# A flow-matching trunk layer on one core: 64 instead of 32 latent tokens served from gathered expert rows, with the low parts, gate chunks and one number row rearranged

## The chip, the cores and the metric

The kernel is written for Trainium2 and runs on one core. The metric is the device time of one execution in microseconds, median of several. The profile is one further execution, with one row for each instruction of each engine: PE (TensorE matmuls), PEld (its weight loads), DVE (VectorE), ACT (ScalarE), POOL (GpSimd) and SP (SyncE, which only issues DMAs).

## What is computed

One trunk layer over 128 context tokens and 512 latent tokens of width 1024, then a final norm: a recurrent and a pooling branch, merged and projected, then a "PEER" channel mixer that picks, for each token, 128 of 16,384 experts (8 heads, 16 each). The mixer is what the change touches:

```
e = (take_along_axis(i1, ci // 16) * 128 + take_along_axis(i2, ci % 16))     # 8 heads x 16 experts a token
g = softmax(sc)
ub = take(u_tab, eb)                       # (token, 128, 1024)
act = gelu(einsum('cd,ced->ce', xb, ub))
vb = take(v_tab, eb)
out = einsum('ce,ced->cd', gbk * act, vb)
```

## The kernel before, in words

All activations lie feature by feature, tokens along the free axis. After the mixer the program goes through these stages:

**Queries and scores** (to about 697 us): 16 blocks of `wq`, scores against the keys, and on VectorE a top-16 `search` for each pair of head (8) and tile of 128 tokens (5), with a `select` that turns indices into expert numbers.

The experts are then served in two ways. *Gathered*: for the 128 context tokens and the first `KS` = 32 latent tokens the rows of the chosen experts are fetched by indirect DMA. A gather fetches one row of 4 KB for each of 128 partitions (512 KB). A context token takes one partition and 128 gathers; the 32 latent tokens are laid four slots to a gather, and take 32 more. So `NG` = 160 gathers of `u_tab` rows, each followed on VectorE by a dot product with the token (`dots`, `early_dots`), and later 160 gathers of `v_tab` rows, each added with its weight to a sum (`weigh`). *Dense*: for the other `TD` = 480 latent tokens all 16,384 experts are computed, 128 at a time, and what was not chosen gets a gate of zero.

**U stage.** For each of 128 blocks of experts (`expert_scores`) PE runs 24 matmuls: 8 slices of the contraction times three products (high x high, low x high, high x low: numbers are split in a high and a low part). ACT rounds the raw weights to the high part (`w_hi`), and POOL or DVE makes the low part `wLo` (`low`). ACT puts a GELU on the result and writes it to a scratch tensor in HBM (`gelu_out`: `gel_d`, two buffers of `gel`, each refilled only when its previous write has landed). A block n's `w_hi` is made as block n-2 ends.

- The first `U1` = 68 blocks run while DVE still searches. POOL makes their low parts, and between them issues the first `D1` = 80 gathers, in program order: 4 gathers to 3 blocks. A gather waits until the row buffer (one of `UR` = 8) has been dotted. DVE puts dots between the pieces of the search.
- Then ACT does the softmax's exponential, DVE the rest of it, PE transposes the expert numbers. 
- In the last `U2` = 60 blocks PE also builds the dense gates: `gates_of` multiplies for each token two one-hot matrices (`ohA`, `ohB`, from `one_hots` on DVE), 8 tokens to a block. ACT copies the result to `stage`, and after 8 blocks (a chunk of 64 tokens) writes 4 MB to HBM (`gate_scratch`), on the same queue as its GELU writes. Six chunks go to HBM; the last 12 blocks' gates (96 tokens) stay in `stage`. DVE here makes the low parts too, and dots 4 rows for 3 blocks, while POOL only issues gathers, up to 8 rows ahead.

**V stage.** For each of 128 blocks DVE multiplies GELUs (`gsr`) and gates (`gates4`, and `stage` for what was kept), ACT and DVE split the product into high and low, and PE again runs 24 matmuls of 480 columns (`values`) that add up in PSUM. DVE also adds 5 gathered rows to 4 blocks.

**The end:** sums, residual, final norm.

Queues: SP loads raw weights (512 KB a block, four buffers), and in the V stage GELUs and gates. ACT's queue writes GELUs and gate chunks. POOL's queue gathers.

Of the kernel before, what the change touches and what calls it, by code (L numbers as in the profile page):

```python
# [152 lines left out]
def build(nc, xT, posT, cT, vecs_d, iota_d, invc_d, gw_d, pw_d, keys_d, wblk, ublk, u_tab, v_tab, ident_d, iota128_d, gel_d, gate_d, yT, st_out):  # L153
# [25 lines left out]
    gates4 = [sb("gates4a", [128, 6, 4, 64])]  # L179
# [21 lines left out]
    same = sb("same", [128, KS])  # L201
# [5 lines left out]
    gates4.append(sb("gates4b", [128, 6, 4, 64]))  # L207
# [86 lines left out]
    iotaP, i1P = P[3][:, 1, 0:16], P[3][:, 1, 16:16 + SLOTS].rearrange("p (a c) -> p a c", a=2)  # L294

# [69 lines left out]
    def _(sp_):  # L365
# [45 lines left out]
        def gate_rows(i, half, n):  # L411

            sp_.dma_start(gates4[half][:, :, :, :].rearrange("p c n t -> p c (n t)"),
                          gate_out[0:6, :, ds(i * 8 + n, 4), :].rearrange("c p n t -> p c (n t)")).then_inc(gt_ld[half], 16)
# [3 lines left out]
        for h in range(2):  # L418
            sp_.wait_ge(gate_st[h], 16 * 3)
            sp_.wait_ge(gel_st[h], 16 * 2)  # L420
# [38 lines left out]
    def _(pool):  # L459
# [45 lines left out]
        with pool.Fori(0, D1 // 16) as i:  # L505
            for b in range(12):
                low(i, 12, 8 + b)
                for g in range(b * 4 // 3, (b + 1) * 4 // 3):
                    if g % 8 == 0:
                        indices(i, 2, i * 16 + g, g // 8, 0, 8, g // 8 + 1)  # L510
                    gather(i, 16, g + 1, g % UR, g // 8, g % 8, u_tab)
        with pool.Fori(0, (SLOTS - D1) // 16) as i:
            for g in range(16):
                if g % 8 == 0:
                    indices(i, 2, i * 16 + (D1 + g), g // 8, 0, 8, (D1 + g) // 8 + 1)
                gather(i, 16, D1 + g + 1, g % UR, g // 8, g % 8, u_tab)
        pool.wait_ge(s["e_ready"], 2)
        for seq in range(SLOTS, NG):
            if seq % 8 == 0:
                indices(0, 0, seq, seq // 8 % 2, 0, 8, seq // 8 + 1)  # L520
            if seq < NG - 16:
                gather(0, 0, seq + 1, seq % UR, seq // 8 % 2, seq % 8, u_tab)
            else:
                gather(0, 0, seq + UR - VR + 1, seq % VR, seq // 8 % 2, seq % 8, u_tab)
        with pool.Fori(0, NE // 16) as i:
            for half in range(2):
                indices(i, 4, i * 16 + half * 8, half, 0, 8, 0, last=False)
                indices(i, 4, i * 4 + (SLOTS + half * 2), half, 8, 2, NG // 8 + half * 2 + 2)
                for g in range(8):
                    v = half * 10 + g + g // 4  # L530
# [1306 lines left out]
```

## Time and profile before

| | |
|---|---|
| time, median of 3 runs | 2189.85 us (2189.37 to 2190.43) |
| the profiled execution: time, and span from first to last instruction | 2194.28 us, 2192.5 us |
| mean granted TensorE clock | 0.979 of full speed |
| busy: PE, PEld, DVE, ACT, POOL | 96%, 86%, 74%, 36%, 33% |
| chain that ended last, by engine | PE 78%, DVE 13%, DMA 3%, issue 3%, ACT 2% |

The chain follows the work back from the last instruction to what released it each time, so its shares say where time was decided, while the busy shares are averages over stages that have different limits. Matmul records overlap one another, so the time from one matmul to the next is read from counts in a stretch or from the chain, not from a row's mean.

### The profile page before, as it was taken

The page shows a single profiled execution, that of the slowest core. Times are in us where ns is not written, and L with a number is a line of the kernel's source. Part 1 is how long each engine was busy: PE and PEld are TensorE (multiplying, and loading weights), DVE is VectorE, ACT ScalarE, POOL GpSimd, SP SyncE. Part 2 cuts the span into 40 slices and gives each one's busy share as a digit, 9 for nine tenths or more (in the row PEclk, how much of TensorE's full clock was granted, in tenths as well). Part 3 has the DMA queues.
Part 4 walks back from the last instruction along what each step waited for, and adds up shares of the span by engine and source line. Part 5 has one row for each costly group of instructions (what it writes and reads, how often), then busy time and mean ns, then how long its engine had stood idle before and what let it go on. Part 6 is the DMA issues. An engine that isn't in the chain of part 4 may idle for free.

```text
span 2192.5 us, 34766 instructions
## 1 busy us (share of the span) xinstructions
PE 2111.8 (96%) x11708; PEld 1879.1 (86%) x11708; DVE 1630.6 (74%) x3336; ACT 799.9 (36%) x1046; POOL 725.6 (33%) x524
## 2 busy tenths in 40 slices
PE   6889998999999999999999999999999999999998
PEld 2889998998899888778888889888888888888887
DVE  4539998242589599993788888887777777777787
ACT  2435555222423322222454445553232323232322
POOL 1223232323133666667422122121222322332331
PEclk8899999999899999999999999999999999999998
DMA  9211222434412688878877677677989989889893
GB/s 368 96 54 58 68 63 68 183 126 169 168 59 78 216 283 279 260 243 284 289 285 285 248 272 292 227 279 245 320 302 313 312 309 367 307 310 317 305 339 115
DMA packets 167482, 502.10 MB, mean 229 GB/s; under 512 B 16608, under 2 KB 74336, under 8 KB 165600
## 3 DMA queue, kind: packets, MB, share of 16 engines
q1 hardware_dynamic: 101872, 273.96, 36.5%
q0 software_dynamic: 46080, 167.79, 22.2%
q10 hardware_dynamic: 19440, 59.25, 6.8%
q8 instruction: 43, 0.70, 0.1%
q14 instruction: 47, 0.39, 0.1%
HBM read 436.45 MB, written 64.50 MB: 228 GB/s over the span
## 4 chain that ended last, share of the span: by engine, by line
PE 78%; DVE 13%; DMA 3%; issue 3%; ACT 2%; SPq 1%; POOL 0%; ACTq 0%; DVEq 0%; POOLq 0%
PE P L840 30%; PE P L557 22%; PE P L751 17%; PE P L775 4%; DMA gel_scratch<-gel 2%; PE P L654 1%; DVE rows L1524 1%; DVE rowsX L1524 1%; PE P L580 1%; DVE oh L1555 1%; DVE oh L1562 1%; DVE keysel L1566 1%; PE P L716 1%; PE P L612 1%; DMA modraw<-in_wblk 1%
## 5 line engine op out<-in xcount | busy, mean ns | idle before, releaser
L864 ACT ACTIVATE wHi<-raw 128x1024 fp32r<-128x1024 f32 x330 | 346.3, 1049 | 1219.9 <-PE P L840 459.4
L751 PE MATMUL P<-hHi,wHi 128*128 128x480 f32 x1024 | 396.1, 387 | 10.8 <-POOL wLo L479 8.1
L751 PE MATMUL P<-hLo,wHi 128*128 128x480 f32 x1024 | 389.3, 380 | 0.0
L751 PE MATMUL P<-hHi,wLo 128*128 128x480 f32 x1024 | 389.1, 380 | 0.0
L1631 DVE TENSOR_TENSOR wLo<-raw,wHi 128x1024 fp32r<-128x1024 f32 x188 | 230.2, 1225 | 167.0 <-ACT wHi L864 162.6
L473 POOL TENSOR_TENSOR wLo<-raw,wHi 128x1024 fp32r<-128x1024 f32 (+1 forms) x76 | 185.2, 2437 | 453.9 <-ACT wHi L864 446.6
L496 POOL DMA_INDIRECT rows<-in_v_tab,Eg x160 | 175.2, 1095 | 468.6 <-DVE accB L1679 225.4
L557 PE MATMUL P<-hHi,wHi 128*128 128x320 f32 x960 | 229.1, 320 | 18.9 <-DVE hLo L1216 14.0
L751 PEld LDWEIGHTS P<-hHi,wHi 128*128 128x128 f32 x1024 | 193.5, 189 | 43.8 <-issue 15.8
L557 PE MATMUL P<-hLo,wHi 128*128 128x320 f32 x960 | 221.1, 311 | 0.0
L557 PE MATMUL P<-hHi,wLo 128*128 128x320 f32 x960 | 220.8, 311 | 0.0
L751 PEld LDWEIGHTS P<-hHi,wLo 128*128 128x128 f32 x1024 | 193.0, 189 | 30.2
L751 PEld LDWEIGHTS P<-hLo,wHi 128*128 128x128 f32 x1024 | 193.5, 189 | 28.2
L840 PE MATMUL P<-wfHib,wLo 128*128 128x480 f32 x512 | 195.0, 381 | 0.0
L840 PE MATMUL P<-wfLob,wHi 128*128 128x480 f32 x512 | 194.9, 381 | 0.0
L840 PE MATMUL P<-wfHia,wHi 128*128 128x480 f32 x512 | 194.2, 379 | 0.0
L840 PE MATMUL P<-wfHib,wHi 128*128 128x480 f32 x512 | 194.1, 379 | 0.0
L840 PE MATMUL P<-wfHia,wLo 128*128 128x480 f32 x512 | 193.5, 378 | 0.0
L840 PE MATMUL P<-wfLoa,wHi 128*128 128x480 f32 x512 | 192.3, 376 | 0.0
L479 POOL TENSOR_TENSOR wLo<-raw,wHi 128x1024 fp32r<-128x1024 f32 x68 | 163.5, 2404 | 79.7 <-ACT wHi L864 79.3
L557 PEld LDWEIGHTS P<-hHi,wHi 128*128 128x128 f32 x960 | 162.9, 191 | 25.4 <-issue 16.5
L496 POOL DMA_INDIRECT rows<-in_u_tab,Eg x88 | 94.8, 1077 | 235.8 <-DVE rows L1524 169.9
(250 smaller groups left out, 3761.2 us busy)
## 6 DMA issues: line engine op xcount, KB each, us to landing
raw<-in_ublk SPq DMA_DIRECT2D x128, 512.0 KB
raw<-in_v_tab SPq DMA_DIRECT2D x128, 512.0 KB
raw<-in_wblk SPq DMA_DIRECT2D x104, 512.0 KB
gel_scratch<-gel ACTq DMA_DIRECT2D x128, 240.0 KB
gsr<-gel_scratch SPq DMA_DIRECT2D x128, 240.0 KB
gate_scratch<-stage ACTq DMA_DIRECT2D x6, 4096.0 KB
gates4a<-gate_scratch SPq DMA_DIRECT2D x16, 768.0 KB
gates4b<-gate_scratch SPq DMA_DIRECT2D x16, 768.0 KB
```

The lines of the kernel that those rows point to most:

```text
L473: pool.tensor_tensor(wLo[:, g % 2, 0:kk], raw[:, r, 0:kk], wHi[:, g % 2, 0:kk].bitcast(f32), ALU.subtract).then_inc(raw_used[r], 1)
L479: pool.tensor_tensor(wLo[:, n % 2, :], raw[:, n % 4, :], wHi[:, n % 2, :].bitcast(f32), ALU.subtract).then_inc(raw_used[n % 4], 1)
L496: pool.indirect_dma_start(out=row(n), out_offset=None, in_=tab, in_offset=bass.IndirectOffsetOnAxis(ap=Eg[:, buf, at:at + 1], axis=0)).the ...
L557: last = nc.tensor.matmul(P[g % 2][:, h, 0:HALF], w_[:, g % 2, k * 128:(k + 1) * 128], cols(x_, k, h), start=(st and a == 0 and b == 0), s ...
L580: last = nc.tensor.matmul(parts_of(m)[32 * j:32 * j + 32, :], c32[:, k, :], raw[:, n % RAW, k * 128:(k + 1) * 128], start=(a == 0), stop=( ...
L612: last = nc.tensor.matmul(P[r // 4][0:2, r // 2 % 2, r % 2 * 256:r % 2 * 256 + 256] .rearrange("p (a n) -> p a n", a=2), cvec[:, 2 * k:2 * ...
L751: last = nc.tensor.matmul(P[0][:, j % 2, 0:TD], w_[:, j % 2, k * 128:(k + 1) * 128], x_[:, k, C0:T], start=(k == 0 and a == 0 and b == 0), ...
L775: last = nc.tensor.matmul(P[1][:, q, n * 128:(n + 1) * 128], ohB[:, q, n, :], ohA[:, q, n, :], start=True, stop=True)
L840: last = nc.tensor.matmul(P[k // 2][:, k % 2, 0:TD], w_[:, j % 2, k * 128:(k + 1) * 128], x_[j % 2][:, :], start=(first and a == 0 and b = ...
L864: return nc.scalar.activation(out, in_, f, **kw)
L1524: V.scalar_tensor_tensor(out=row(b), in0=row(b), scalar=1.0, in1=vec, op0=ALU.mult, op1=ALU.mult, accum_out=actv[:, ds(i * per + n, 1)]).t ...
L1631: V.tensor_tensor(wLo[:, n % 2, :], raw[:, n % 4, :], wHi[:, n % 2, :].bitcast(f32), ALU.subtract).then_inc(raw_used[n % 4], 1)
```

## The change

- `KS` goes from 32 to 64, so 448 latent tokens stay dense instead of 480. The 64 are laid two slots to a gather: 64 gathers instead of 32 for each table, `NG` = 192.
- `U1`/`U2` go from 68/60 to 72/56, `D1` from 80 to 96. POOL issues 3 gathers to 2 blocks in the first part.
- In the second part the low parts move from DVE to POOL, which alternates them with the gathers; the loops are written out. DVE there builds one-hots and dots only (96 dots in 56 blocks).
- The row of numbers 0 to 127 that `ohB` compares with is read from PSUM (`iota128P`, in bank P3); the token vectors are read from PSUM (`htokP`, P2) to the last dot, so the first matmul of the V stage that writes P2 waits for `act_ready`, which DVE gives after the last dot.
- Seven chunks of gates; five go to HBM, the last two (chunks 5 and 6, 128 tokens) stay whole in `stage`.
- In the search, dots start after the second tile's row numbers and not after the first's; then 2 follow each unit (before 1 and 2 in turn), and 5 lie in each `select` (before 3).

```diff
-KS = 32
+KS = 64
-U1, U2 = 68, 60
+U1, U2 = 72, 56
-D1 = 80
-KEPT = 48
+D1 = 96
+CH, CK = 7, 5
...
-        with pool.Fori(0, D1 // 16) as i:
-            for b in range(12):
-                low(i, 12, 8 + b)
-                for g in range(b * 4 // 3, (b + 1) * 4 // 3):
+        with pool.Fori(0, D1 // 48) as i:
+            for b in range(32):
+                low(i, 32, 8 + b)
+                for g in range(b * 3 // 2, (b + 1) * 3 // 2):
...
+        for b in range(U2):
+            low(0, 0, U1 + b)
+            for seq in range(D1 + b * (NG - D1) // U2, D1 + (b + 1) * (NG - D1) // U2):
+                if seq == SLOTS:
+                    pool.wait_ge(s["e_ready"], 2)
...
             for k in ((4, 5, 6, 7, 2, 3, 0, 1) if first else range(KC)):
+                if first and k == 4:
+                    pe.wait_ge(s["act_ready"], 1)
...
+        def gates_of_chunk(c):
+
+            half = (c + 1) % 2
+            if c >= 2:
+                act.wait_ge(gate_st[half], c // 2 * 16)
+            if c < CK:
+                with act.Fori(0, 2) as i:
+                    for j in range(4):
+                        gate_block(i + c * 2, j, half, i * 32 + j * 8)
+                act.wait_ge(s["bank_free"], c * 16 + 18)
+                act.dma_start(gate_in[c, :, :], stage[:, half, :, :].rearrange("p n t -> p (n t)")
+                              ).then_inc(gate_st[half], 16)
+            else:
+                for b in range(8):
+                    gate_block(c * 2 + b // 4, b % 4, half, b * 8)
...
             search(n, unit, before)
-            early_dots(1 + n % 2)
+            early_dots(2)
...
         dotted[1] = D1
-        early_dots(4)
-        low(0, 0, P_U + U1, 0)
-        early_dots(2)
-        low(0, 0, P_U + U1, 1)
-        with dve.Fori(0, (SLOTS - D1) // 16) as i:
-            one_hots(i, htokP)
-        one_hots(3, htok2[:, :])
-        one_hots(4, htok2[:, :], final=True)
+        early_dots(6)
+        for b in range(U2):
+            one_hots(b)
+            for n in range(D1 + b * (NG - D1) // U2, D1 + (b + 1) * (NG - D1) // U2):
+                late_dot(n)
...
         def weighs(i, c):
 
-            weigh(i, c + c // 4, acc if c % 2 == 0 else accB, wgt[:, ds(i * 16 + c, 1)])
-            if c % 4 == 3:
-                weigh(i, c + c // 4 + 1, acc2, wgt[:, ds(i * 4 + (SLOTS + c // 4), 1)])
+            weigh(i, c + c // 2, acc if c % 2 == 0 else accB, wgt[:, ds(i * 16 + c, 1)])
+            if c % 2 == 1:
+                weigh(i, c + c // 2 + 1, acc2, wgt[:, ds(i * 8 + (SLOTS + c // 2), 1)])
```

What the code above makes of the engines' order is seen at two places. On POOL, at the end of the first part of the U stage, the program before leaves the low parts (`wLo`) and goes on with gathers alone (`rows` and `rowsX` are the row buffers, `Eg` the expert numbers of the next eight gathers):

```order
L479 TENSOR_TENSOR wLo<-raw,wHi 128x1024
...
L489 COPY Eg<-E 128x8
L496 DMA rows<-in_u_tab,Eg 128x1024 x4
L496 DMA rowsX<-in_u_tab,Eg 128x1024 x4
L489 COPY Eg<-E 128x8
```

The changed program goes on with a low part for each block, and one or two gathers behind it:

```order
L482 TENSOR_TENSOR wLo<-raw,wHi 128x1024
L492 COPY Eg<-E 128x8
L499 DMA rows<-in_u_tab,Eg 128x1024
L482 TENSOR_TENSOR wLo<-raw,wHi 128x1024
L499 DMA rows<-in_u_tab,Eg 128x1024 x2
L482 TENSOR_TENSOR wLo<-raw,wHi 128x1024
L499 DMA rows<-in_u_tab,Eg 128x1024
L499 DMA rowsX<-in_u_tab,Eg 128x1024
L482 TENSOR_TENSOR wLo<-raw,wHi 128x1024
```

So a gather is now issued behind the low part of its own block, and no longer as soon as a buffer is free. On DVE, at the same place, stood before, between the copies of the transposed numbers and the first one-hot (`P` is PSUM, `actv` the dot's result):

```order
L1625 COPY keysel<-P 128x2x512
L1626 COPY SC<-P 128x512
L1524 SCALAR_TENSOR_TENSOR rows,actv<-rows,P 128x1024 x2
L1524 SCALAR_TENSOR_TENSOR rowsX,actv<-rowsX,P 128x1024 x2
L1631 TENSOR_TENSOR wLo<-raw,wHi 128x1024
L1524 SCALAR_TENSOR_TENSOR rowsX,actv<-rowsX,P 128x1024 x2
L1631 TENSOR_TENSOR wLo<-raw,wHi 128x1024
```

Now there stands:

```order
L1629 COPY keysel<-P 128x2x512
L1630 COPY SC<-P 128x512
L1525 SCALAR_TENSOR_TENSOR rows,actv<-rows,P 128x1024 x2
L1525 SCALAR_TENSOR_TENSOR rowsX,actv<-rowsX,P 128x1024 x4
L1643 TENSOR_TENSOR ohB<-P,keysel 128x512
L1646 TENSOR_SCALAR ohA<-iota,keysel,SC 128x128 x4
L1643 TENSOR_TENSOR ohB<-P,keysel 128x512
L1646 TENSOR_SCALAR ohA<-iota,keysel,SC 128x128 x4
L1525 SCALAR_TENSOR_TENSOR rows,actv<-rows,P 128x1024
```

The low parts are gone from DVE, the six dots are the same, and each block is two groups of one-hots and then its one or two dots.

## Rows read from the trace of the kernel before

**Rows 1.** Windows by stage (U first, U second, V): stretch; busy us (instructions) of PE, PEld, DVE, ACT, POOL; clock; DMA share; GB/s.
```profile
697.00:1074.00 377.00, 366.18 (x1667) 312.69 (x1666) 300.07 (x878) 109.84 (x144) 244.73 (x167) 0.99 0.78 258
1074.00:1502.00 428.00, 419.41 (x2377) 375.82 (x2376) 360.51 (x813) 212.47 (x239) 92.58 (x86) 0.99 0.72 265
1502.00:2168.00 666.00, 666.00 (x3069) 575.84 (x3069) 506.25 (x678) 200.28 (x260) 194.81 (x187) 1.00 0.89 308
```

**Rows 2.** Chain in order of time (start, us, what), U stage.
```profile
1067.43 7.01 PE P L751 x24
...
1225.63 1.78 PE P L775 x16
...
1241.39 5.22 PE P L751 x24
...
1248.32 15.31 DMA gel_scratch<-gel
...
1272.20 5.20 PE P L751 x24
...
1411.93 5.22 PE P L751 x24
...
1441.60 5.20 PE P L751 x24
```

**Rows 3.** Windows of PE for line L557 (320 columns): busy (matmuls), busy (loads).
```profile
200.00:300.00 100.00, 87.65 (x580) 85.41 (x580) 1.00 0.21 67
```

**Rows 4.** Windows of all engines, first part of U.
```profile
720.00:860.00 140.00, 140.00 (x648) 121.16 (x647) 113.08 (x310) 41.01 (x54) 95.77 (x64) 1.00 0.78 262
860.00:1000.00 140.00, 131.86 (x587) 110.21 (x587) 134.03 (x419) 36.44 (x48) 90.43 (x62) 0.99 0.81 259
```

**Rows 5.** POOL's gathers: two of the timeline, and their group in the page.
```profile
738.09 1.12 POOL L496 DMA_INDIRECT rows<-in_u_tab,Eg  x1 [1.14 <-issue]
...
947.02 0.94 POOL L496 DMA_INDIRECT rows<-in_u_tab,Eg  x1 [6.62 <-DVE rows L1524]
...
L496 POOL DMA_INDIRECT rows<-in_u_tab,Eg x88 | 94.8, 1077 | 235.8 <-DVE rows L1524 169.9
```

**Rows 6.** Timeline of ACT, second part of U (L1176 writes a gate chunk).
```profile
1186.55 1.06 ACT L864 ACTIVATE wHi<-raw 128x1024 fp32r<-128x1024 f32 x1 [2.72 <-PE P L751]
...
1244.09 0.34 ACTq L1176 DMA_DIRECT2D gate_scratch<-stage  x1
...
1265.12 0.57 ACT L864 ACTIVATE gel<-P 128x480 f32<-128x480 f32 x1 [3.40 <-issue]
```

**Rows 7.** Windows with the most DMA traffic: second part of U, V.
```profile
1245.00:1260.00 15.00, 15.00 (x86) 13.49 (x85) 12.72 (x32) 7.06 (x8) 2.54 (x2) 1.00 0.99 396
1808.00:1840.00 32.00, 32.00 (x149) 27.68 (x148) 23.70 (x34) 9.32 (x12) 8.88 (x9) 1.00 1.03 402
```

**Rows 8.** Timeline of DVE: its first dot, and a block of the second part.
```profile
743.83 1.22 DVE L1524 SCALAR_TENSOR_TENSOR rows<-rows,P 128x1024 f32<-128x1024 f32 x1 [20.77 <-DMA rows<-in_u_tab,Eg]
...
1190.02 0.69 DVE L1639 TENSOR_TENSOR ohB<-iota,keysel 128x512 f32<-128x512 f32 x1 [1.16 <-ACT stage L864]
1190.63 1.11 DVE L1643 TENSOR_SCALAR ohA<-iota,keysel,SC 128x128 f32<-128x128 f32 x4
...
1193.29 1.21 DVE L1524 SCALAR_TENSOR_TENSOR rowsX<-rowsX,P 128x1024 f32<-128x1024 f32 x1
...
1194.43 1.22 DVE L1524 SCALAR_TENSOR_TENSOR rowsX<-rowsX,P 128x1024 f32<-128x1024 f32 x1
```

**Rows 9.** Timeline: two DVE operations of like size, and a low part on POOL.
```profile
713.62 0.18 DVE L1547 SCALAR_TENSOR_TENSOR abf<-abf 128x16 f32<-128x16 f32 x1
713.83 2.29 DVE L1549 TENSOR_TENSOR ab<-abf 128x16 uint32<-128x16 f32 x1
...
713.68 2.40 POOL L479 TENSOR_TENSOR wLo<-raw,wHi 128x1024 fp32r<-128x1024 f32 x1 [2.79 <-ACT wHi L864]
```

**Rows 10.** Timeline of DVE, V stage.
```profile
1607.96 1.23 DVE L1631 TENSOR_TENSOR wLo<-raw,wHi 128x1024 fp32r<-128x1024 f32 x1 [1.61 <-ACT wHi L864]
```

More of the change, by code:

```diff
@@ L200, in build @@
     stfin = sb("stfin", [128, 2, KC])
-    same = sb("same", [128, KS])
+    same = sb("same", [128, 32])
+    sameK = sb("sameK", [128, KS])
     sp = sb("sp", [128, 16])
@@ L799, in context_sums @@
             for k in range(KC):
-                last = nc.tensor.matmul(P[1][:, 0, k * KS:(k + 1) * KS], acc2[:, k * 128:(k + 1) * 128], same[:, :],
+                last = nc.tensor.matmul(P[1][:, 0, k * KS:(k + 1) * KS], acc2[:, k * 128:(k + 1) * 128], sameK[:, :],
                                         start=True, stop=True)
@@ L1568, in select @@
             ins.then_inc(s["head_done"], 1)
+            early_dots(1)
         def row_numbers(t, selects):
@@ L1603, in _ @@
                         dve.sem_inc(s["row_free"], UR)
-                        dotted[1] = 70
+                    else:
+                        dotted[1] = D1 - 12
             before = unit
@@ L1632, in low @@
                             ).then_inc(raw_used[n % 4], 1)
-        def one_hots(i, vec, final=False):
-            for b in range(12):
-                for q in range(2):
-                    dve.wait_ge(s["bank_free"], i * 24 + (b * 2 + q + 1))
-                    c = i * 96 + (C0 + b * 8 + q * 4)
-                    V.tensor_tensor(ohB[:, q, :, :], iota128[:, :].unsqueeze(1).broadcast_to([128, 4, 128]),
-                                    keysel[:, 1:2, ds(c, 4)].rearrange("p a n -> p (a n)").unsqueeze(2).broadcast_to(
-                                        [128, 4, 128]), ALU.is_equal)
-                    for n in range(4):
-                        last = V.tensor_scalar(ohA[:, q, n, :], iota128[:, :],
-                                               keysel[:, 0:1, ds(c + n, 1)].rearrange("p a n -> p (a n)"),
-                                               SC[:, ds(c + n, 1)], ALU.is_equal, ALU.mult)
-                    last.then_inc(s["oh_ready"], 1)
-                for g in range(b * 4 // 3, (b + 1) * 4 // 3):
-                    dots(i, 16, D1 + g, vec)
-                if not (final and b >= 10):
-                    low(i, 12, P_U + U1, b + 2)
@@ L1652, in _, with one_hots @@
-        dotted[1] = D1
-        early_dots(4)
-        low(0, 0, P_U + U1, 0)
-        early_dots(2)
-        low(0, 0, P_U + U1, 1)
-        with dve.Fori(0, (SLOTS - D1) // 16) as i:
-            one_hots(i, htokP)
-        one_hots(3, htok2[:, :])
-        one_hots(4, htok2[:, :], final=True)
+        def one_hots(b):
+            for q in range(2):
+                dve.wait_ge(s["bank_free"], b * 2 + q + 1)
+                c = C0 + b * 8 + q * 4
+                V.tensor_tensor(ohB[:, q, :, :], iota128P.unsqueeze(1).broadcast_to([128, 4, 128]),
+                                keysel[:, 1, c:c + 4].unsqueeze(2).broadcast_to([128, 4, 128]), ALU.is_equal)
+                for n in range(4):
+                    last = V.tensor_scalar(ohA[:, q, n, :], iota128[:, :], keysel[:, 0, c + n:c + n + 1],
+                                           SC[:, c + n:c + n + 1], ALU.is_equal, ALU.mult)
+                last.then_inc(s["oh_ready"], 1)
```

95 lines of the change are left out of this document (40 added, 55 removed).

## The prediction, made before the change was run

> **What bounds the kernel now.** I read the windows by stage first [rows 1]. PE is busy without a gap in the V stage (666 of 666 us), and in 97 and 98% of the two parts of the U stage. These stages are two thirds of the span, and PE ends them. In their chain there is a steady beat of 24 expert matmuls in 5.20 us, and in the second part of U 16 one-hot matmuls in 1.78 us beside them [rows 2]. So an expert matmul of 480 columns takes 216.7 ns from one to the next.
>
> The gaps come second. From 697 to the first one-hots at 1074.4 (the end of the slow block that starts at 1067.43 [rows 2]) lie 69 blocks, 358.8 us at 5.20; it took 377. Between 860 and 1000 PE did 587 matmuls where 140 us hold 648 [rows 4]: 61 x 0.2167 = 13 us lost. The timeline says how: a gather on POOL waits for a dot on DVE, 6.6 us in the row [rows 5], and the low part behind the gather is late. About 4 of the other 5 us are at the switch to one-hots, where that slow block waited for a low part that DVE owed behind four dots (7.01 us for 24 matmuls). In the second part of U, 60 x 1.78 + 59 x 5.20 = 413.6 us became 428 [rows 1]: 14.4 lost. After a 4 MB gate write ACT's next GELU write lands 15.3 us after its issue [rows 2], and the GELU that needs this buffer waits 3.4 us [rows 6]. Four beats of 6.98 are 27.9 us; around two gate writes they are 30.8 and 29.7 [rows 2].
>
> **The columns.** The change removes 32 of 480 columns from 6,144 matmuls. No row has 448 columns, so I bound the price by 320: 87.65 us for 580 matmuls, 151.1 ns each [rows 3]. The slope is (216.7 - 151.1)/160 = 0.41 ns a column, hence 203.6 ns at 448 (4.89 us a block), and 13.1 ns x 6,144 = **-80.6 us**. The end above is in proportion to the columns: 216.7 x 32/480 = 14.4 ns, -88.8 us. That loads of weights set a floor near 200 ns is excluded, since 320 columns run faster.
>
> **The one-hots.** 56 blocks instead of 60, at 1.78 [rows 2]: **-7.1 us**.
>
> **The first part of U.** POOL must now issue 3 gathers in 2 x 4.89 us instead of 4 in 3 x 5.20: one each 3.26 us, before 3.90. DVE has to dot at that rate, for POOL is at most 8 rows ahead. DVE is full here (134 of 140 us [rows 4]), and by the program it gets 64 dots instead of 54 before the end of the search: 10 x 1.14 us (from one dot to the next [rows 8]) = 11.4 us more. But before, its first dot waited 20.8 us for the first gather [rows 8], since it was asked for too early; now DVE does the second tile first, and that wait is gone. So the search ends some 9 us sooner, while PE is sooner by 50 blocks x 0.31 = 16 us. The balance is about as tight as before: I leave the 13 us where they are (**0**), with -10 to +12 as ends. ACT comes to the exponential when it did (64 x 5.20 = 333 us, 68 x 4.89 = 333 us in). At the switch the low part is POOL's and no dots stand before it; but six dots (6.9 us) and one group of one-hots (1.6) have to fit in two blocks (9.8 us), which leaves 1.3 us for two copies of 1024 and 512 elements, which at the dots' 1.2 ns an element are 1.8. I take 2 us where 4 were: **-2**.
>
> **The second part of U.** DVE sheds a low part (1.2 us a block) and gets 1.71 dots instead of 1.33 (+0.4): 3.27 for its one-hots [rows 8] and 1.71 x 1.14 make 5.2 us of a beat of 6.67, so it isn't the bound; nor is POOL with 2.4 [rows 9] + 1.71 x 1.08 [rows 5] = 4.2 us. What gets worse is the collision with a gate write. A block's traffic without GELUs is 512 KB of weights and 1.71 gathers, 1.42 MB in 6.67 us = 213 GB/s, before 1.22 MB in 6.98 = 175. All queues together moved 396 and 402 GB/s in the fullest windows [rows 7], in the mean 399. The 4.19 MB of a write and the GELU block behind it (0.25, now 0.23 MB) then need 4.44/(0.399 - 0.175) = 19.8 us before, and the trace has 1248.3 + 15.3 - 1244.1 = 19.5 [rows 2, 6]. Now it is 4.42/(0.399 - 0.213) = 23.8 us, if the others keep their pace, while the buffer is wanted 0.6 us sooner. So the wait of 3.4 becomes up to 8 us, and less as a stalled PE asks for less: I take 6. A second wait stands beside it: gathers were issued up to 8 rows (6 blocks) ahead of their dot, and now 8 to 9 us ahead (behind the low part of block n, made as n-2 ends; the dots of n follow one-hots made after n-1 ended). Alone a gather took 743.8 - 738.1 = 5.7 us [rows 5, 8]; behind a gate write it may be as late as a GELU write, 15 us. DVE then stands for some us, at the same time as ACT. I take 6 us for each of 5 writes, 30 us, instead of 9 (of the 14.4; the rest I give to the last gates before V, which keep it): **+21 us**. The ends are +3 (2.4 each, as in the stretches seen) and +40.
>
> **The V stage.** DVE adds 1.5 rows a block instead of 1.25. It waits 1.61 us of a block for ACT's high part when it has one row to add [rows 10]; a second row (1.2 us) comes in each 2nd block and not each 4th, so 0.1 to 0.2 us are left in those when the beat is 4.89, and 1.4 in the others. Two buffers even this out. DMA: 512 + 224 + 160 + 768 KB in 4.89 us are 348 GB/s, before 1584 KB in 5.20 = 312 (308 with the edges [rows 1]). The same stage carried 402 GB/s for 32 us and PE lost nothing (149 matmuls, 215 ns each [rows 7]). So it fits; for bursts I take **+4 us** (0 to +30). The new wait for the last dot at the start of V is covered: after its last gates PE has 4.9 us of one more block, and two dots take 2.3.
>
> The Trainium skill (DMA: Bandwidth & Descriptors, Specifications) puts the limit of one core's HBM traffic at about 358 GB/s; by that rule 348 in V would just fit, and the sum would be the same there, while a gate write would need 4.42/(0.358 - 0.213) = 30 us (an estimate) and each of the 5 waits some 6 us more. The windows at 396 and 402 GB/s disagree with the limit.
>
> **The sum.** -80.6 - 7.1 - 2 + 21 + 4 = **-65 us**. From the profiled execution's 2194.3 this gives 2129; the median is 4.4 lower, so I predict **2125 us**, with 2100 (columns in proportion, small collisions) to 2148 (the worst collisions) for this case alone. Changes under about 0.2% (4 us) can't be told from none.
>
> **The rivals.**
>
> *Waits don't grow* (0.15): collisions stay at 9 us and V at 0. That is -90, 2100. For it: most writes cost little before. Against it: the gathers' shorter lead.
>
> *DMA becomes the bound of V* (0.13). Its share is 0.89 at 308 GB/s [rows 1], in proportion it is full at 346, and 1664 KB (1.70 MB) take 4.93 us a block; with bursts 5.0 to 5.1, +14 to +27 on the sum, 2139 to 2152. Against it: share 1.03 at 402 GB/s [rows 7].
>
> *The gathers' lead is too short in ordinary blocks too* (0.12). Then DVE waits for rows, and PE for `ohA`, in each of 56 blocks; at 0.5 us that is +28, 2153. Against it: 5.7 us of 8.
>
> *Slower: DVE and POOL shut each other out* (0.05). Beside a low part a DVE operation like one of 0.18 us took 2.29, and both ended at 716.1 [rows 9]. Low parts now run beside one-hots in each block. By the rows a low part lies from 1.1 to 3.5 us after a block's end (behind 1.06 of `wHi`), and the first `ohA` starts at 1190.6 - 1186.5 = 4.1 [rows 6, 8]: they miss each other by 0.6 us. If gathers push the low part back, a block pays up to 2.4 us; with 1 us of slack on DVE that is 1.4 x 56 = +78, 2203. It decides from 1.2 us of PE's time a block (65/56).
>
> The Trainium skill (SBUF — State Buffer, the table of ports and its consequences) says that both engines share a pair of ports as an exclusive lock, which VectorE needs for two inputs in SBUF or a double-rate mode; by that rule an `ohA` that comes during a low part waits for its end, as the rows of 716.1 agree, and a dot with its vector in PSUM doesn't.
>
> *The change doesn't do what it says* (0.01): something else holds the beat at 5.2; then -7 - 2 + 21 + 4 are left, 2206.
>
> The forecast has 0.54. The first four cases make 0.94, of which I leave 0.02 to "within 0.2%"; faster 0.92, slower 0.06. The range 2100 to 2153 leaves out the slower cases, half of the first rival and the tails of the second and third, 2 in 10.
>
> **What the new profile would show.** In the chain 24 matmuls in 4.89 us (5.2 would refute the first term) and 16 in 1.78. Some 60 matmuls missing around the search's end, with POOL waiting for dots. After each of five gate writes an ACT wait before a GELU, and a DVE wait for gathered rows; none there, and the collision term is wrong; DVE waits between writes speak for the third rival. In V PE without gaps at a DMA share of 0.95 or more; waits for `wLo` or `wfLo` speak for the second. `ohA` rows of over 1 us each speak for the slower case.

## The result and the profile after

The changed kernel takes 2155.5 us (median of 4 runs, 2153.2 to 2160.1) beside 2189.6 of the kernel before on the same chip: a ratio of 0.985 (0.983 to 0.986), 34 us faster where the prediction had 65. Its profiled execution took 2157.4 us, with a span of 2155.6. In all that follows two executions are left out, one of 7040.9 us of e6_spread_switch and one of 4222.1 us of the kernel before beside it.

Windows of the kernel after, by stage, with the columns of [rows 1]:

```profile
693.00:1076.00 383.00, 365.98 (x1773) 329.16 (x1771) 329.49 (x900) 115.08 (x155) 271.41 (x185) 1.00 0.82 275
1076.00:1495.00 419.00, 385.40 (x2215) 360.18 (x2216) 304.05 (x754) 196.93 (x223) 225.31 (x165) 0.95 0.75 276
1495.00:2134.00 639.00, 634.43 (x3103) 582.57 (x3101) 539.24 (x725) 198.44 (x262) 232.33 (x220) 0.99 0.93 337
```

PE was busy in 98% of the second part of U before and is in 92% now, at a granted clock of 0.95 where it was 0.99. Where it waits, the groups of PE's matmuls say (busy us, mean ns, idle before and what ended it):

```profile
L752 PE MATMUL P<-hHi,wHi 128*128 128x448 f32 x1024 | 383.6, 375 | 16.3 <-POOL wLo L482 13.1 <-ACT gel L867 3.2
L776 PE MATMUL P<-ohA,ohB 128*128 128x128 f32 x896 | 120.2, 291 | 34.3 <-DVE ohA L1646 34.3
L843 PE MATMUL P<-wfHib,wHi 128*128 128x448 f32 x512 | 190.0, 371 | 4.6 <-DVE wfLob L1712 4.6
```

The middle row is the result in short. Before the change that wait was 8.6 us:

```profile
L775 PE MATMUL P<-ohA,ohB 128*128 128x128 f32 x960 | 120.9, 279 | 8.6 <-DVE ohA L1643 8.6
```

Its place is in the chain of the kernel after (start, us, what), at two of the five gate writes:

```profile
1132.25 0.95 POOL rowsX L499
...
1134.32 16.70 DMA rows<-in_u_tab,Eg
1151.04 1.23 DVE rows L1525 x2
1152.27 0.60 DVE ohB L1643
1152.87 1.03 DVE ohA L1646 x4
1153.91 0.04 issue
1153.95 3.56 PE P L776 x16
1157.52 4.95 PE P L752 x24
...
1164.25 4.90 PE P L752 x24
...
1192.93 15.93 DMA rowsX<-in_u_tab,Eg
...
1210.72 2.93 DVE ohA L1646 x4
```

ACT issued the gate write at 1132.8. A gather issued beside or behind it lands 16 to 18 us after its issue (15.9 to 17.9 at the five writes, and the chain runs through such a gather at each). DVE holds its dot for it, the next one-hots stand behind the dot, and PE behind the one-hots. DVE's waits for gathered rows between 1090 and 1500, and ACT's for the `gel` buffer (us in total, times, longest):

```profile
DVE rowsX L1525 <- DMA rowsX<-in_u_tab,Eg: 20.9, 4, 6.6
DVE rows L1525 <- DMA rows<-in_u_tab,Eg: 20.1, 6, 7.2
...
ACT gel L867 <- DMA gel_scratch<-gel: 7.5, 5, 1.8
```

The same chain has the first terms of the sum: 24 matmuls in 4.90 us (5.20 before [rows 2]), and, where no wait stands before them, 16 one-hot matmuls in 1.78.

For all kernels below I read one table from the traces: the three stages by their first matmuls (U, first one-hot matmul, V, last V matmul) and PE's idle time in them. "Ideal" is the beat without a loss: in the first part 69 blocks of 5.20 us before and 73 of 4.89 after, and 1.3 us of transposes; in the second 59 x 5.20 + 60 x 1.78 before and 55 x 4.89 + 56 x 1.78 after; 128 blocks in V.

| kernel | median us | first part | second part | V | PE idle, U blocks / one-hots / V |
|---|---|---|---|---|---|
| ideal before, ideal after | | 360.1, 358.3 | 413.6, 368.6 | 665.6, 625.9 | |
| before | 2189.6 | 377.7 | 428.2 | 669.3 | 10.8 / 8.6 / 0 |
| after | 2155.5 | 382.3 | 419.5 | 638.1 | 16.3 / 34.3 / 4.6 |
| e1_tiny | 2119.8 | 385.7 | 379.4 | 638.2 | 16.3 / 6.8 / 4.2 |
| e2_spread | 2120.7 | 383.2 | 380.3 | 632.3 | 16.5 / 7.4 / 0.8 |
| e3_lead | 2152.9 | 386.4 | 415.6 | 633.7 | 16.5 / 28.0 / 2.3 |
| e4_olddots | 2178.6 | 406.5 | 419.3 | 632.7 | 30.5 / 34.8 / 1.2 |
| e5_switch | 2153.0 | 381.6 | 413.2 | 638.7 | 15.8 / 30.7 / 5.4 |
| e6_spread_switch | 2114.9 | 382.7 | 376.8 | 637.6 | 16.1 / 3.8 / 5.1 |
| e7_tail | 2154.9 | 384.8 | 419.3 | 631.8 | 15.9 / 34.6 / 0.8 |
| e8_dvelow | 2131.4 | 386.2 | 390.2 | 634.1 | 18.9 / 12.8 / 2.6 |
| e9_pace80 | 2147.8 | 366.3 | 425.6 | 637.5 | 1.8 / 41.8 / 4.6 |
| e10_before_spread | 2184.6 | 377.6 | 421.1 | 669.3 | 10.6 / 3.9 / 0 |
| e11_spread_dvelow | 2116.9 | 386.6 | 379.1 | 632.7 | 18.6 / 4.1 / 1.2 |
| e12_best | 2094.6 | 366.9 | 377.3 | 630.9 | 1.8 / 4.2 / 0.2 |
| e13_sbufrow | 2099.8 | 367.0 | 377.1 | 637.1 | 1.8 / 3.8 / 4.5 |
| e14_oldtail | 2097.1 | 367.0 | 377.5 | 632.8 | 1.8 / 4.2 / 1.1 |

A stage is read from one execution, a median from 4 to 6. Executions of one kernel with the change differ by 2 to 14 us, so a few microseconds of a median settle nothing, and the table is read where a stage moves by more than its neighbours do. The traced execution of e2_spread was its fastest, at 2112.6 us 8 under its median, so its three stages are those of a good execution.

### The profile page after: what moved, and what is told of

Read it like the earlier page. It is cut to its first block, busy times and chain, and to the rows that moved or that the text cites. A ratio compares the mean times of both kernels' runs of the same rounds, so it can differ in the third digit from the quotient of the medians.

```text
span 2155.6 us, 34251 instructions
## 1 busy us (share of the span) xinstructions
PE 2039.9 (95%) x11644; PEld 1880.8 (87%) x11644; DVE 1632.2 (76%) x3330; ACT 784.1 (36%) x1037; POOL 920.1 (43%) x652
## 4 chain that ended last, share of the span: by engine, by line
PE 70%; DVE 17%; DMA 6%; issue 3%; ACT 2%; POOL 1%; SPq 1%; ACTq 0%; DVEq 0%; POOLq 0%
PE P L843 28%; PE P L558 22%; PE P L752 12%; PE P L776 3%; DMA rows<-in_u_tab,Eg 2%; DVE rowsX L1525 2%; DVE rows L1525 2%; DMA rowsX<-in_u_tab,Eg 2%; PE P L655 1%; DVE cand L1512 1%; DVE ohA L1646 1%; DVE oh L1564 1%; PE P L581 1%; DVE keysel L1568 1%; DVE oh L1557 1%
## 5 line engine op out<-in xcount | busy, mean ns | idle before, releaser
L752 PE MATMUL P<-hHi,wHi 128*128 128x448 f32 x1024 | 383.6, 375 | 16.3 <-POOL wLo L482 13.1
L752 PE MATMUL P<-hLo,wHi 128*128 128x448 f32 x1024 | 377.0, 368 | 0.0
L752 PE MATMUL P<-hHi,wLo 128*128 128x448 f32 x1024 | 377.0, 368 | 0.0
L558 PE MATMUL P<-hHi,wHi 128*128 128x320 f32 x960 | 227.7, 318 | 18.9 <-DVE hLo L1216 13.9
L1635 DVE TENSOR_TENSOR wLo<-raw,wHi 128x1024 fp32r<-128x1024 f32 x128 | 156.8, 1225 | 87.7 <-ACT wHi L867 81.7
L843 PE MATMUL P<-wfHib,wHi 128*128 128x448 f32 x512 | 190.0, 371 | 4.6 <-DVE wfLob L1712 4.6
L843 PE MATMUL P<-wfLob,wHi 128*128 128x448 f32 x512 | 189.8, 371 | 0.0
L843 PE MATMUL P<-wfHib,wLo 128*128 128x448 f32 x512 | 189.5, 370 | 0.0
L843 PE MATMUL P<-wfHia,wHi 128*128 128x448 f32 x512 | 187.1, 365 | 0.0
L843 PE MATMUL P<-wfHia,wLo 128*128 128x448 f32 x512 | 187.0, 365 | 0.0
L843 PE MATMUL P<-wfLoa,wHi 128*128 128x448 f32 x512 | 186.8, 365 | 0.0
L558 PEld LDWEIGHTS P<-hHi,wHi 128*128 128x128 f32 x960 | 161.8, 190 | 25.1 <-issue 16.1
L1681 DVE SCALAR_TENSOR_TENSOR htok<-rows,wgt,htok 128x1024 f32<-128x1024 f32 x128 | 163.6, 1278 | 8.6 <-DMA rows<-in_v_tab,Eg 8.6
```

The lines of the kernel that those rows point to most:

```text
L558: last = nc.tensor.matmul(P[g % 2][:, h, 0:HALF], w_[:, g % 2, k * 128:(k + 1) * 128], cols(x_, k, h), start=(st and a == 0 and b == 0), s ...
L752: last = nc.tensor.matmul(P[0][:, j % 2, 0:TD], w_[:, j % 2, k * 128:(k + 1) * 128], x_[:, k, C0:T], start=(k == 0 and a == 0 and b == 0), ...
L843: last = nc.tensor.matmul(P[k // 2][:, k % 2, 0:TD], w_[:, j % 2, k * 128:(k + 1) * 128], x_[j % 2][:, :], start=(first and a == 0 and b = ...
L1635: V.tensor_tensor(wLo[:, n % 2, :], raw[:, n % 4, :], wHi[:, n % 2, :].bitcast(f32), ALU.subtract).then_inc(raw_used[n % 4], 1)
L1681: V.scalar_tensor_tensor(out=into[:, :], in0=rows[:, n % VR, :], scalar=weight, in1=into[:, :], op0=ALU.mult, op1=ALU.add).then_inc(s["row ...
```

## The experiments

All are edits of the changed kernel, except e10; e13 and e14 are edits of e12.

### The gate write: taken away, cut, or met with a longer lead

e1_tiny leaves 15/16 of each gate write out, and V reads the part that is written for every key, so that its results are other ones and its reads as large as before:

```diff
-                act.dma_start(gate_in[c, :, :], stage[:, half, :, :]...
+                act.dma_start(gate_in[c, :, 0:512], stage[:, half, 0:8, :]...
```

> This kernel leaves out most of the gates' way through HBM: of each of the five chunks only 1/16 of the 4.19 MB is written (keys 0 to 7), and V reads these keys' gates for every key, the same number of bytes as before, so its numbers are other ones and nothing else moves. Theory A (a 4 MB gate write delays whatever is asked for behind it, gathers above all; it costs about 8 us of PE five times, 46.6 us lost in the second part of U): that part falls from 415.8 to about 377 us (ideal 369.2), no gather takes over 8 us there, and the time falls by 35 to 42 us from 2155.5 to 2114 to 2120. Theory B (the loss is DVE's or POOL's own: dots, one-hots and low parts in each other's way): the part stays above 405 us and the time above 2145. Rival C (the gathers' lead of 8 to 9 us is too short by itself): DVE still waits for rows in ordinary blocks, a part of 385 to 400 us, 2125 to 2140.

2119.8 us, ratio 0.968 (0.966 to 0.969). The second part fell from 419.5 to 379.4 us: 40.1 us for five writes, **8.0 each**. Theory A holds, B and C fall: without the write DVE waits for a row once in the whole second part (1.0 us), so the lead of 8 us is enough in an ordinary block.

e2_spread writes all bytes, in eight pieces, one to a block of the next chunk (ACT's loops are written out for it):

```diff
+        def gate_piece(c, k):
+            half = (c + 1) % 2
+            act.dma_start(gate_in[c, :, k * 1024:(k + 1) * 1024],
+                          stage[:, half, k * 16:(k + 1) * 16, :]...).then_inc(gate_st[half], 16)
...
+            if 1 <= c <= CK and b < 7:
+                if b == 0:
+                    act.wait_ge(s["bank_free"], (c - 1) * 16 + 18)
+                    gate_piece(c - 1, 7)
+                gate_piece(c - 1, b)
```

> The same bytes as the changed kernel, but each gate write is cut into 8 pieces of 512 KB: 7 are issued one in each of the next chunk's first blocks, with the eighth at its head. By theory A (a burst of 4.19 MB keeps the transfers behind it for 16 to 18 us) a piece keeps them for at most 2 to 3 us, which the lead of 8 us covers: the second part of U takes 372 to 382 us, and the time is 2114 to 2125. By theory D (it is the sum of bytes in this stretch that is too much, not the burst) the loss stays at about 40 us, only spread over all blocks: 2145 to 2160. ACT issues 35 DMAs more, at most 1 us each beside other work: 0 to 5 us slower in either case if that matters.

2120.7 us, ratio 0.969 (0.968 to 0.971); the second part took 380.3 us, as without the bytes. Theory D falls. The same traffic costs 8 us a write in one DMA, and in eight spread over eight blocks no more than without the bytes. (Eight pieces issued at once weren't tried, so it is not shown that cutting without spreading would do.) The group of the one-hot matmuls in this trace:

```profile
L776 PE MATMUL P<-ohA,ohB 128*128 128x128 f32 x896 | 112.2, 277 | 7.4 <-DVE ohA L1650 7.2
```

e3_lead issues gathers earlier:

```diff
-            for seq in range(D1 + b * (NG - D1) // U2, D1 + (b + 1) * (NG - D1) // U2):
+            for seq in range(issued(b), issued(b + 1)):   # n + 5, at most NG - 16
```

> Only the gathers' lead is changed: in the second part of U POOL issues each gather up to 5 rows (3 blocks) earlier than in the changed kernel, as far as the 8 row buffers allow. If the lateness of a gathered row is what PE pays for at a gate write (chain: gather, dot, one-hot, matmul), the lead of 8 us grows to 20 us or more, above the 16 to 18 us that a gather takes there: the second part of U falls by 25 to 40 us, 2115 to 2130. If the GELU write behind the gate write would end the wait next, as the prediction had it (15 us from issue, a buffer wanted after 12), only 5 to 15 us come back: 2140 to 2150. If POOL's low part then comes late, because a gather in front of it waits for a dot, the time doesn't fall at all: 2150 to 2165.

2152.9 us, ratio 0.983 (0.981 to 0.986): by its time the third case, with the wait of the second in it, and an instructive one. DVE's wait for rows is gone (1.5 us, once), and the second part still took 415.6. The chain of e3_lead says what came in its place:

```profile
1121.46 3.18 DVE ohA L1651 x4
1124.64 0.60 DVE ohB L1648
1125.24 3.21 DVE ohA L1651 x4
...
1145.71 14.18 DMA gel_scratch<-gel
...
1176.30 3.29 DVE ohA L1651 x4
```

Two things. The GELU write behind a gate write, 14 us, ends the wait now. And four `ohA` take 3.2 us instead of 1.03, since the low part, queued on POOL behind gathers that wait for a dot, now falls on them; an `ohA` takes 433 ns in the mean over the kernel, 365 in the changed one ([rows 9] has such a pair). POOL's gathers, which stand in front of its low parts, waited 45.9 + 40.5 us for dots. The lead was bought with the low part's punctuality.

### The low parts on DVE again

```diff
         for b in range(U2):
-            low(0, 0, U1 + b)          # POOL
...
+            if b < U2 - 2:
+                low(0, 0, P_U + U1, b + 2)   # DVE, behind the dots
```

> The low parts of the second part of U are made on DVE behind the dots again, as before the change, and POOL only issues gathers, up to 8 rows ahead. If the gathers' short lead came from the low parts on POOL and is what a gate write costs, DVE no longer waits for rows at a write, while DVE has 5.2 + 1.2 us of a beat of 6.67: a part of 375 to 395 us instead of 415.8, 2120 to 2135. By what the kernel with only a longer lead showed (DVE's waits for rows went from 41 to 1.5 us and the time hardly moved, since the GELU buffer behind the write was waited for next), each write still costs 4 to 6 us: 395 to 410 us, 2135 to 2150. If DVE at 6.4 of 6.67 us is too full, every block pays: over 2155.

2131.4 us, ratio 0.973 (0.971 to 0.975), in the first of its ranges. The second part took 390.2 us: of the 40 us at the writes 29 are due to this one part of the change. POOL, free of low parts, runs its gathers the full eight rows ahead, and DVE waits for none. What is left at a write is the wait that the prediction was about, in the chain of e8_dvelow:

```profile
1130.81 4.92 PE P L751 x24
...
1137.40 14.13 DMA gel_scratch<-gel
...
1157.33 1.16 PE P L775 x8
1158.48 4.91 PE P L751 x24
```

From 1130.81 to 1158.48 PE does four blocks (96 matmuls and 64 of the one-hots), 26.7 us by the beat and 27.7 by the rows: 1 us lost here, 4 at the next write, 2 or 4 at the others.

> Cut writes and the low parts of the second part of U on DVE again. With whole writes the low parts on DVE took 24 us off (the part from 419.5 to 390.2 us between the first one-hots and V). If they cost nothing but the gathers' lead at a burst, then without bursts there is nothing left to gain: 2118 to 2124 like the 2120.7 of cut writes alone, and DVE's fuller beat (6.4 of 6.67 us) may cost up to 5 us. If low parts on POOL also cost PE in ordinary blocks (one-hots held up by the shared port), 2112 to 2117.

2116.9 us, ratio 0.966 (0.965 to 0.968). By that it is at the upper end of the second case, but e2_spread, 4 us above it, has runs from 2112.6 to 2126.6, and by the traces it is the first: the second parts are 379.1 and 380.3 us. So the four kernels make a square, second part of U:

| | whole writes | cut writes |
|---|---|---|
| low parts on POOL (the change) | 419.5 | 380.3 |
| low parts on DVE | 390.2 | 379.1 |

The low part on POOL costs 29 us beside bursts and 1 without; a burst costs 39 us with it and 11 without. Alone they cost 1 and 11 us, together 40.

### The bursts in the kernel before

The same cut in the kernel before, six writes:

> The kernel before the change, with its six gate writes cut into 8 pieces of 512 KB in the same way, and nothing else. It is the base of a comparison without bursts: the changed kernel with cut writes takes 2120.7. If all of what the change's second part of U lost over the prediction is the burst, then between these two kernels the prediction's other terms hold: columns and one-hots -88, first part and switch +3, V +4 to +7, that is -76 to -81, and this kernel takes 2197 to 2202, slower than before. The trace of before gives the opposite sign: it lost 14.4 us in its second part, some 9 of them at writes, so 2178 to 2184, and then the change is worth only -58 to -63 without bursts and something else is missing from my account.

2184.6 us, ratio 0.997 (0.996 to 0.998); the second part went from 428.2 to 421.1 us. A gate write cost 7.1/6 = **1.2 us** before the change and 8.0 after it.

The time lies just above the second case, and that case's consequence holds: without bursts the change is worth 2184.6 - 2120.7 = 64 us by the medians (61 by the two ratios), and not 76 to 81, so the burst is not all that the sum had wrong. Between the two traces the first part gets 5.6 us longer, the second 40.8 shorter and V 37.0 shorter; the ideals have 1.8, 45.0 and 39.7 shorter, so some 7, 4 and 3 us are lost in the three stages even without bursts.

### The pace of gathers and dots in the first part of U

```diff
-D1 = 96
+D1 = 80
...
-        with pool.Fori(0, D1 // 48) as i:
-            for b in range(32):
-                low(i, 32, 8 + b)
-                for g in range(b * 3 // 2, (b + 1) * 3 // 2):
+        for b in range(64):
+            low(0, 0, 8 + b)
+            for g in range(b * 5 // 4, (b + 1) * 5 // 4):
```

> Only the share of the gathers is changed: 80 of the 192 in the first part of U (5 in 4 blocks, one each 3.9 us as before the change) and 112 in the second (2 a block), where the changed kernel has 96 (3 in 2 blocks) and 96. If the pace of the gathers is what cost PE the 18 us between 800 and 1000, then 5 to 12 us come back there. Against it stand 0.3 gathers a block more in the second part, whose five writes cost 8 us each: 9 or 10 each by the arithmetic of bytes, +5 to +10. So 2148 to 2160 in all; the first part alone tells the theories apart: 386 us as now if DVE's search is the limit and not the pace, 374 to 381 if it is the pace.

2147.8 us, ratio 0.981 (0.979 to 0.984). The first part took 366.3 us, 16 less, more than I had hoped for; the second 425.6, 6 more, as expected. Windows of the kernel after, and then of e9_pace80:

```profile
800.00:900.00 100.00, 92.83 (x443) 82.00 (x442) 98.14 (x311) 26.84 (x36) 71.02 (x50) 1.00 0.84 279
900.00:1000.00 100.00, 92.74 (x447) 82.77 (x446) 92.86 (x249) 28.25 (x38) 73.05 (x52) 1.00 0.85 288
```

```profile
800.00:900.00 100.00, 100.00 (x486) 90.97 (x485) 94.46 (x321) 30.36 (x42) 73.49 (x49) 1.00 0.86 283
900.00:1000.00 100.00, 100.00 (x486) 90.97 (x485) 79.98 (x223) 29.85 (x40) 73.77 (x49) 1.00 0.84 285
```

DVE is 98 and 93% busy in the first pair, with 3 dots in 9.8 us beside the search; 14 us of idle PE are the price. With 5 dots in 19.6 us there is none: PE's matmul count is full, and DVE, at 94 and 80%, has room. This is the pace of the kernel before, where PE waited 8.1 us for late low parts in this part and here 1.8; so the change's other order of the dots did help, and its pace took more away.

e4_olddots takes back the change's order of dots in the search: their density between the units, the two `early_dots(1)` in a selection (not shown here), and their start. Without the `else` the dots begin after the first tile's row numbers again, as before the change:

```diff
-            early_dots(2)
+            early_dots(1 + n % 2)
...
-                    else:
                         dotted[1] = D1 - 12
```

> Only DVE's schedule of dots in the search is as it was before the change: one and two in turn after a search unit, three in a selection instead of five, held back at the same place. If the denser dots are what keeps POOL's gathers in pace, it gets worse: DVE falls behind, PE loses 10 to 20 us more between 700 and 1075 and the time is 2160 to 2175. If the dots only have to be done somewhere and their order doesn't matter, since DVE is full anyway, 2152 to 2158.

2178.6 us, ratio 0.995 (0.994 to 0.997): the first case, and 4 us beyond its upper end. The first part took 406.5 us, 24 more, and PE's wait for low parts in it went from 13.1 to 29.0 us. Without this small edit two thirds of the change's gain are gone: a gather every 3.26 us needs its dot in time, because the low part is behind it on POOL. The 24 us are not those of the density alone, as the expectation takes it. The first dot, at 752.2 us and without a wait in the kernel after, is asked for so early here that DVE stands for its row:

```profile
739.81 1.22 DVE L1525 SCALAR_TENSOR_TENSOR rows<-rows,P 128x1024 f32<-128x1024 f32 x1 [16.13 <-DMA rows<-in_u_tab,Eg]
```

How the 24 us divide between the later start and the denser dots no run tells.

### The switch and the tail of V

```diff
+        one_hots(0)
         early_dots(6)
         for b in range(U2):
-            one_hots(b)
+            if b:
+                one_hots(b)
```

> At the switch from the first to the second part of U the first one-hots are made before the six dots held back for this place, not after them. The switch lost 9.7 us in the changed kernel, where the prediction had 2. If the six dots (6.9 us) and the copies on DVE's way to the first one-hots are the cost, about 5 us come back, 2149 to 2152. If it is POOL's low part, late behind a gather that waits for one of these dots, the dots only come later and PE waits at the next block in its stead: no change, 2153 to 2157.

2153.0 us, ratio 0.983 (0.982 to 0.985), by its time the second case, which the spread of the runs doesn't tell from the changed kernel. The traces do. Chain of the kernel after, then of e5_switch, from the last low part before the switch:

```profile
1056.52 2.39 POOL wLo L482
1058.96 5.08 PE P L752 x24
...
1067.31 2.37 DVE rows L1525 x4
1069.68 4.57 DVE rowsX L1525 x8
...
1076.48 3.16 DVE ohA L1646 x4
1079.68 2.07 PE P L776 x8
1081.76 6.59 PE P L752 x24
1088.35 1.78 PE P L776 x16
```

```profile
1058.51 2.39 POOL wLo L482
1060.95 5.22 PE P L752 x24
...
1067.48 9.91 PE P L752 x48
1077.39 1.78 PE P L776 x16
1079.17 4.90 PE P L752 x24
1084.08 1.78 PE P L776 x16
```

From the low part to the second one-hots it is 31.8 us in the first and 25.6 in the second: 6.3 us less, which is the six dots' 6.9 nearly. The first one-hots come at the same time in both (first parts of 382.3 and 381.6 us), so the 6 us lie in the second part. In the changed kernel the second group's `ohA` meet POOL's next low part and take 3.16 us. With the cut writes the same edit goes with 6 us in the median:

> Both edits that helped by themselves: the gate writes in 8 pieces over the next chunk's blocks, and the first one-hots made ahead of the six dots. Cut writes alone gave 2120.7, one-hots first alone 2.5 us less than the changed kernel. If the two are independent, 2113 to 2118. If with the cut writes the dots that now come after the first one-hots delay the gathers behind them (they had a lead of 8 us), the gain at the switch comes back later: 2119 to 2123.

2114.9 us (2115.7 with the execution that is left out), ratio 0.966 (0.963 to 0.968), the first case.

e7_tail spreads the last rows of V, three in some blocks, over all 16:

> Only the last 16 blocks of V: the rows that DVE adds there, 29 of them with the ones it is behind by, go evenly over the blocks (one or two in each), where the changed kernel adds three in the blocks 3, 7 and 11 of the 16. In its trace a third row waits for its gather, 8 us after its buffer came free, and PE stands for 4.6 us with its clock granted at 0.8 behind it. If this is the tail's loss, PE doesn't wait in V at all and the time falls by 5 to 9 us, 2147 to 2151. If the gathers are late because the DMA queues are full, two rows a block are as late as three: 2153 to 2158.

2154.9 us, ratio 0.984 (0.982 to 0.986). V fell from 638.1 to 631.8 us in the trace, and PE's waits in it from 4.6 to 0.8, but the median, in the second case, didn't move beyond what runs differ by.

### The version that beats both

Cut writes, one-hots first, 80 gathers in the first part, even tail:

> All edits that helped in some stage: cut writes, the first one-hots ahead of the six dots, 80 gathers in the first part of U and 112 in the second, and the even tail of V. Cut writes with one-hots first gave 2115.7. The slower pace took 16 us off the first part by itself (first one-hots at 1060.9 instead of 1075.9) and gave 6 back in the second, at the bursts that are gone here: 2098 to 2102. If 2 gathers a block are too much beside the written pieces, 2102 to 2110. The tail is worth 0 to 5 of it.

**2094.6 us**, ratio 0.956 (0.955 to 0.958): 4.4% under the kernel before. It is below the range I gave it. Two small terms were tried from here. e13_sbufrow gives the second one-hots their row of numbers from SBUF again (`iota128` for `iota128P`), e14_oldtail takes the even tail out.

> The fastest version so far (cut writes, one-hots first, 80 gathers in the first part, even tail; 2094.6) with one part of the change undone: the second one-hots read their row of numbers from SBUF again, not from PSUM. If low parts on POOL and one-hots on DVE shut each other out and the PSUM row is what avoids it, an ohB beside a low part takes 2 to 3 us instead of 0.7: where it hits one in ten of the 112, PE waits for it and the time grows by 3 to 15 us, 2098 to 2110. If they miss each other in time, nothing changes: 2092 to 2097. An ohB row may even be a tenth of a microsecond shorter.

2099.8 us (2092.3 to 2101.2), ratio 0.958 (0.956 to 0.959). By its time it is the first case; but its second part took 377.1 us, as that of e12_best, so the row in PSUM is worth nothing there. The group on DVE, in e12_best and then in e13_sbufrow:

```profile
L1646 DVE TENSOR_TENSOR ohB<-P,keysel 128x512 f32<-128x512 f32 x112 | 77.0, 687 | 57.2 <-ACT stage L866 57.0
```

```profile
L1646 DVE TENSOR_TENSOR ohB<-iota,keysel 128x512 f32<-128x512 f32 x112 | 84.3, 753 | 49.5 <-ACT stage L866 49.0 <-issue 0.5
```

Some `ohB` do get held up with the row in SBUF, by 7 us over 112, and none with it in PSUM (the longest took 1.96 us and 0.69). DVE idles some 50 us ahead of them, so PE sees nothing. The 5 us between the medians come from elsewhere, by the trace from V, which took 637.1 us instead of 630.9: PE waits 4.2 us there for one late gather, though the tail is even.

> The same fastest version without the even tail of V, that is with three rows in the blocks 3, 7 and 11 of the last 16 as in the changed kernel. V took 638.1 us in the changed kernel and 630.9 with the even tail. If the tail costs time, 2098 to 2102, with 3 to 5 us of waits for wfLo at the end of V; if the difference was the state of the clock behind other stages, 2092 to 2097.

2097.1 us (2095.4 to 2103.8), ratio 0.958 (0.957 to 0.960), V at 632.8 us. The tail's 0 to 5 us aren't told apart from the spread. V took 632 to 634 us with the old tail in e2_spread, e3_lead, e4_olddots and e14_oldtail, and 637 with the even one in e13_sbufrow, so a gather comes late in some executions and not in others, whatever the tail.

## Why the prediction was wrong

**The columns and the one-hots: right.** 4.90 us for 24 matmuls, 203.2 ns each (246 in 50 us), against 203.6; -81 us is there, as are the 1.78 us. The ideals take 86.5 us off, where the sum had 87.7.

**The first part of U: wrong, +8.4.** I had the balance "about as tight as before: I leave the 13 us where they are", and -2 at the switch. Over the ideal the stage lost 17.6 us before and 24.0 after, where 15.6 were predicted. The search's share rose, as I counted 16 us of PE against 9 of DVE and then called it even; e9_pace80 and e4_olddots show how steep this place is, -16 us for 5 gathers in 4 blocks instead of 6, and +24 for the old order of dots. At the switch I set six dots and one group of one-hots against two blocks and found them to fit within half a microsecond. They don't: the low part before them was late as well, the second group met a low part (3.16 us), and the block behind ran at a granted clock of 0.72 (6.59 us). e5_switch gets 6.3 us back, which my table counts to the second part, since they are lost behind the first one-hots.

**The second part of U: the step that failed, +15.** The stage lost 14.6 us before and 50.9 after, where 35.6 were predicted. Its sum had 9 us of loss at writes before, and 6 us for each of five now. The runs put 1.2 at each of six before (e10_before_spread), 7 in all, and 8.0 at each now (e1_tiny), 40 in all: +33 where +21 stood. The other 3 of the 15 us are outside the writes, where the switch lies. The prediction named both waits but made the GELU buffer the one that decides, and let the gathers' wait go on "at the same time". It is the other way round: a gather has 8 to 9 us of lead, takes 16 to 18 behind the write, and holds PE for 4.4 to 6.6 us, 5.5 in the mean; most of the other 2.5 of the 8.0 us goes at the low clock behind the wait (16 one-hot matmuls in 3.56 us for 1.78). ACT's waits for `gel` came to 7.5 us in all. The number 6 was read off the wrong transfer and came near PE's wait by luck; what it lacked is the clock. The lead was lost with the move of the low parts to POOL. The prediction saw the short lead and gave it no term of its own, since DVE would stand "at the same time as ACT"; with the low parts on DVE 29 of the 40 us are gone, though ACT waits longer for its buffer there (14.5 us in all in e8_dvelow, 7.5 in the changed kernel).

**V: near in size, another cause, +4.5.** DMA carries 350 GB/s at a share of 0.97 until 2080 with PE full (0.93 and 337 GB/s are the means with the end); the rival in which it bounds V is refuted. The +4 stood for bursts, but the loss came at the end. Chain of the kernel after:

```profile
2079.12 8.24 DMA rows<-in_v_tab,Eg
...
2092.94 7.88 DMA rows<-in_v_tab,Eg
...
2103.86 26.11 PE P L843 x114
```

Each of these gathers starts when a row's buffer comes free and takes 8 us in V, where three rows fall in one block; 114 matmuls then take 26.1 us instead of 23.2, at a granted clock of 0.89.

**The rivals.** The gathers' lead as a cost of each ordinary block was the third; its time, 2153, is nearly what was measured, but by another way: ordinary blocks don't pay (e1_tiny), five writes do. That DVE and POOL shut each other out happened in single places (2.93, 3.16 us) and is a cost of e3_lead, not of the change. The Trainium skill (SBUF — State Buffer, the table of ports and its consequences) has these two engines exclude each other at a port, and a read from PSUM stay clear of it; the rows agree, with 1.03 us for four `ohA` alone and 2.9 to 3.3 in which a low part of 2.4 us lies, and with the longest `ohB` of 1.96 us from SBUF and 0.69 from PSUM.

The terms over the prediction are 8.4 + 15.3 + 4.5 = 28.2 us, and the profiled execution came 28 above the 2129 predicted for it (the ideals give 1.2 us more, and what lies before U and behind V added up to 1.6 us less than before). What stays open: which gather of V comes late in which execution, and how much of the few microseconds between medians is due to it.

Of the signs that I named, the 4.90 and 1.78 us are there, and so are both waits behind each of the five writes. Between 800 and 1000 us some 92 matmuls are missing (890 where 200 us hold 982), and not 60.

## What to carry over

A big write needn't be slower to hurt more: it delays what is asked for behind it, on other queues too (a gather from 5.7 to 16 to 18 us), and what counts is each reader's lead, from its issue to its use. So when work is moved in front of a queue of transfers, price the lead that they lose, not only the engine time; and spread a write of megabytes in pieces between other work, which here was worth 35 us. Where an engine is full (98% here) and another waits for it, a pace faster by a fifth isn't even: going back to the old pace was worth 16 us of that stage.

## What was unexpected of the hardware

- A gather of 512 KB took 5.7 us alone [rows 5, 8], 8.2 and 7.9 near the end of V beside 315 and 309 GB/s, and 16 to 18 behind a write of 4.19 MB, though it is on another queue.
- After a wait of a few microseconds PE ran at its low level for some more. Windows of the kernel after around a write:

```profile
1142.00:1146.00 4.00, 4.00 (x29) 3.79 (x28) 0.00 (x0) 3.29 (x4) 2.79 (x2) 1.00 1.12 468
1146.00:1150.00 4.00, 2.59 (x13) 2.04 (x11) 1.23 (x2) 1.21 (x2) 1.76 (x3) 1.00 0.84 338
1150.00:1154.00 4.00, 0.05 (x1) 0.05 (x1) 2.96 (x8) 0.54 (x1) 3.54 (x3) 0.97 1.03 418
1154.00:1158.00 4.00, 4.00 (x20) 3.95 (x21) 3.42 (x9) 1.40 (x2) 0.45 (x1) 0.61 1.03 416
```

  The 16 one-hot matmuls behind the wait took 3.56 us instead of 1.78, twice as long: 1.2 GHz, not 2.4; over the 4 us around them the granted clock is 0.61. PE's waits at the five writes are 27.5 us, 5.5 each, of a loss of 8.0 (of the 34.3 us in all, 3.3 are at the switch and 3.5 before the last gates). The 468 GB/s of the first row stand at a DMA share of 1.12, more than full, so a window this short reads too high; the four together are 410 GB/s, near the 402 of [rows 7].
- Eight DMAs of 512 KB on ACT's queue, one a block, cost PE nothing that the times show, where one of 4.19 MB cost 8.0 us.
